# Running log-decay sums made once as rows, spread by single 512-column products

## What is computed

```python
# delta rule, per head
gc = jnp.cumsum(g, axis=-1)                      # g = -exp(a_log) * softplus(...)
decay = jnp.exp(jnp.where(causal, gc[..., :, None] - gc[..., None, :], -jnp.inf))
a_in = jnp.einsum("bhnid,bhnjd->bhnij", kb, k) * decay
qk = jnp.einsum("bhnid,bhnjd->bhnij", q, k) * decay
q_dec = q * jnp.exp(gc)[..., None]
...
# scan, per head
acs = jnp.cumsum(jnp.moveaxis(adt_i, 1, -1), axis=-1)
lmat = jnp.exp(jnp.where(causal, acs[..., :, None] - acs[..., None, :], -jnp.inf))
y_diag = jnp.einsum("bgls,bghls,bsghp->blghp", cb, lmat, xdt_i)
```

## Time and profile before

| what | us |
|---|---|
| median of 3 executions | 2161.22 |
| lowest, highest | 2158.73, 2166.72 |
| span of the profiled execution | 2157.8 |
| PE busy in it | 2109.7 (98%) |
| DVE, ACT, POOL busy | 1213.1, 906.3, 325.6 |

### The profile page before, as it was taken

One profiled execution on the slowest core, in us unless ns is written; L12 is line 12 of the kernel. 1 busy time (PEld: TensorE's weight loads), 2 busy tenths in 40 slices (PEclk: granted clock), 3 DMA queues, 4 the chain that ended last, 5 costly groups with the idle time before them and its releaser, 6 DMA issues.

```text
span 2157.8 us, 26841 instructions
## 1 busy us (share of the span) xinstructions
PE 2109.7 (98%) x9776; PEld 1698.0 (79%) x9776; DVE 1213.1 (56%) x1663; ACT 906.3 (42%) x1282; POOL 325.6 (15%) x266
## 2 busy tenths in 40 slices
PE   6999999999999999999999999999999999999999
PEld 5778888878868888877766888888878878888887
DVE  5898755765366665226544566653354465666522
ACT  6883445434254444224564444442242354444311
POOL 0002121220122222001302122210000011222100
PEclk9999999999999999999999999999999999999999
DMA  7323322122323233221111333232222122323321
GB/s 234 93 77 92 86 74 69 59 69 69 101 65 97 94 94 120 94 86 59 59 40 50 97 94 94 95 116 96 80 77 88 51 78 88 98 97 97 114 94 66
DMA packets 81481, 188.96 MB, mean 88 GB/s; under 512 B 19824, under 2 KB 40432, under 8 KB 81392
## 3 DMA queue, kind: packets, MB, share of 16 engines
q1 hardware_dynamic: 81392, 187.75, 27.6%
HBM read 178.28 MB, written 9.44 MB: 87 GB/s over the span
## 4 chain that ended last, share of the span: by engine, by line
PE 92%; DVE 4%; ACT 2%; issue 1%; DMA 0%; POOL 0%; SPq 0%; ACTq 0%; DVEq 0%; POOLq 0%
PE acc L253 23%; PE acc L255 23%; PE acc L254 23%; PE bank L1726 1%; PE bank L1245 1%; PE bank L229 1%; PE bank L230 1%; PE bank L231 1%; PE acc L2634 1%; PE acc L2633 1%; PE acc L2632 1%; PE bank L2017 1%; PE bank L253 1%; PE bank L255 1%; PE bank L254 1%
## 5 line engine op out<-in xcount | busy, mean ns | idle before, releaser
L253 PE MATMUL acc<-HH,whi 128*128 128x512 f32 x1600 | 642.1, 401 | 7.1 <-DVE wlo L191 4.5
L255 PE MATMUL acc<-HH,wlo 128*128 128x512 f32 x1600 | 624.4, 390 | 0.0
L254 PE MATMUL acc<-HL,whi 128*128 128x512 f32 x1600 | 623.5, 390 | 0.0
L185 ACT ACTIVATE whi<-raw 128x1024 fp32r<-128x1024 f32 (+1 forms) x293 | 324.2, 1108 | 573.5 <-PE acc L255 543.4
L191 DVE TENSOR_TENSOR wlo<-raw,whi 128x1024 fp32r<-128x1024 f32 (+1 forms) x293 | 400.9, 1369 | 287.8 <-ACT whi L185 287.8
L253 PEld LDWEIGHTS acc<-HH,whi 128*128 128x128 f32 x1600 | 301.1, 188 | 74.1 <-DVE wlo L191 11.0
L255 PEld LDWEIGHTS acc<-HH,wlo 128*128 128x128 f32 x1600 | 300.5, 188 | 64.0
L254 PEld LDWEIGHTS acc<-HL,whi 128*128 128x128 f32 x1600 | 301.1, 188 | 62.0 <-issue 4.1
L253 PE MATMUL acc<-FH,whi 128*128 128x512 f32 x528 | 208.9, 396 | 0.0
L255 PE MATMUL acc<-FH,wlo 128*128 128x512 f32 x528 | 208.6, 395 | 0.0
L254 PE MATMUL acc<-FL,whi 128*128 128x512 f32 x528 | 208.5, 395 | 0.0
(11 more groups left out here) (394 smaller groups left out, 2673.1 us busy)
## 6 DMA issues: line engine op xcount, KB each, us to landing
raw<-w SPq DMA_DIRECT2D x257, 512.0 KB, 3.5
raw<-w SPq DMA_DIRECT2D x48, 704.0 KB, 4.0
X<-x SPq DMA_DIRECT2D x4, 512.0 KB, 5.2
x_dram<-small SPq DMA_DIRECT2D x8, 256.0 KB, 4.4
xt_dram<-small SPq DMA_DIRECT2D x8, 256.0 KB, 3.6
a_dram<-l_am SPq DMA_DIRECT2D x8, 256.0 KB, 3.7
l_xt<-xt_dram SPq DMA_DIRECT2D x8, 256.0 KB, 3.5
l_x<-x_dram SPq DMA_DIRECT2D x8, 256.0 KB, 3.3
```

The lines of the kernel that those rows point to most:

```text
L185: nc.scalar.activation(hi[:, 0:kt * P], raw[u % RAW][:, 0:kt * P], ACT.Copy).then_inc(w_hi_ready, 1)
L253: nc.tensor.matmul(a[:, :], wh, tile(hi, k), start=start and k == 0, stop=False)
L254: nc.tensor.matmul(a[:, :], wh, tile(lo, k), start=False, stop=False)
L255: last = nc.tensor.matmul(a[:, :], wl, tile(hi, k), start=False, stop=stop and k == kt - 1)
```

## The change

The running sums of all 24 heads are made once, as rows. DVE writes `t_ld4`, which holds each chunk's 24 log-decay columns four times (signs -, -, +, + on the factor), POOL having zeroed it first. PE multiplies its four 128-column chunks by `upper` into `bank[5]` in the middle of the second unit of h = 1 (new L1448, four float32 128x128 products). ACT rounds the result into `rows_r` (fp32r); DVE replaces rows 32-63 and 96-127 of it with the remainders, so that a row and the row 32 below it add up to a sum in two rounded parts.

- Delta rule: L1764's four float32 products become one fp32r product of 512 columns, with `pick_r` (ones at rows p and 32+p) as stationary operand.
- Scan: POOL's `sd_u` becomes the chunk's rows times a selector of the head (`row_of`), with rows 64-127 set to one; the stationary operand is `sd_left` (ones above, the negative rows below). L2508's eight products become two of 512 columns. They give the difference of the sums with a sign that is not yet clamped, so ACT takes Abs from PSUM into `sd_e` and then Exp with scale -1, where it took one Exp.
- Once, ahead of the scan, POOL makes `row_of` in two steps and sets two memsets, and ACT copies half of `rows_r` to `sd_left`.
- The constant table is loaded in two pieces of 3 and 5 blocks of 128 columns instead of one of 13; seven thresholds on semaphores move with it.

The core of the diff:

```diff
+            dve.wait_ge(g_zero, 1)
+            for r, sign in enumerate((-1.0, -1.0, 1.0, 1.0)):
+                nc.vector.scalar_tensor_tensor(out=t_ld4[:, :].rearrange("p (c r n) -> p c r n", c=NC, r=4)[:, :, r, 0:24],
+                                               in0=by_chunk(t_soft)[:, :, 8:32], scalar=sign,
+                                               in1=t_neg[:, :].unsqueeze(1).to_broadcast([P, NC, 24]),
+                                               op0=ALU.mult, op1=ALU.mult).then_inc(a_dve, 1)
+
+        def rows_pe(pe):
+            pe.wait_ge(a_dve, 8)
+            for k in range(NC):
+                last = nc.tensor.matmul(chunk(bank[5], k), chunk(t_ld4, k), upper, start=True, stop=True)
+            last.then_inc(a_pe, 1)
+
+        def rows_act(act):
+            act.wait_ge(a_pe, 6)
+            nc.scalar.activation(rows_r[:, :], bank[5][:, :], ACT.Copy).then_inc(a_steps, 1)
+
+        def rows_dve(dve):
+            dve.wait_ge(a_steps, 9)
+            for r in (slice(32, 64), slice(96, 128)):
+                nc.vector.tensor_tensor(rows_r[r, :], bank[5][r, :], rows_r[r, :].bitcast(F32), ALU.subtract).then_inc(a_dve, 1)
...
+                if p == 0:
+                    rows_act(act)
                 act.wait_ge(unit_done, u0 + 2 * h + 2)
...
                     beta_exp_dve(dve)
+                    rows_dve(dve)
...
-                    unit(2 + 2 * h)
+                    unit(2 + 2 * h, 0)
+                    unit(2 + 2 * h, 1)
+                    rows_pe(pe)
+                    unit(2 + 2 * h, 2)
+                    unit(2 + 2 * h, 3)
                     pe.wait_ge(a_steps, 8)
...
-                    pe.wait_ge(a_dve, 4)
+                    pe.wait_ge(g_zero, 3)
+                    pe.wait_ge(a_dve, 11)
...
-                for k in range(NC):
-                    last = nc.tensor.matmul(chunk(bank[2], k), head_col(t_ld, 24 * k, p).to_broadcast([P, P]), upper,
-                                            start=True, stop=True)
-                last.then_inc(p_prod, 1)
+                nc.tensor.matmul(bank[2][:, :], pick_r[:, p:p + 1].to_broadcast([P, P]), rows_r[:, :],
+                                 start=True, stop=True).then_inc(p_prod, 1)
...
-                    nc.scalar.activation(sd_e[q][:, :], bank[q][:, :], ACT.Exp).then_inc(d_e, 1)
+                    nc.scalar.activation(sd_e[q][:, :], bank[q][:, :], ACT.Abs).then_inc(d_abs, 1)
+                for q in range(2):
+                    act.wait_ge(d_abs, 2 * n + q + 2)
+                    nc.scalar.activation(sd_e[q][:, :], sd_e[q][:, :], ACT.Exp, scale=-1.0).then_inc(d_e, 1)
...
-                    nc.gpsimd.tensor_tensor(by_chunk(sd_u[q]), of_heads(t_ld, 24 * k + 8 + 8 * g + 4 * q, 4, P),
-                                            each_chunk(lower), ALU.mult).then_inc(d_u, 1)
+                    h0 = 8 + 8 * g + 4 * q
+                    nc.gpsimd.tensor_tensor(by_chunk(sd_u[q]), each_chunk(chunk(rows_r, k).bitcast(F32)),
+                                            of_heads(row_of, h0, 4, P), ALU.mult).then_inc(d_u, 1)
...
-                    for j in range(4):
-                        last = nc.tensor.matmul(chunk(bank[q], j), chunk(sd_u[q], j), upper, start=True, stop=True)
-                    last.then_inc(d_d, 1)
+                    nc.tensor.matmul(bank[q][:, :], chunk(sd_left, k), sd_u[q][:, :], start=True, stop=True).then_inc(d_d, 1)
```

More of the change, by code:

```diff
@@ L95, in program @@
         ident, ones, upper, lower, halves = (cst[:, k * P:(k + 1) * P] for k in range(5))
-        neg_lower, neg_ones, hidden = (cst[:, k * P:(k + 1) * P] for k in range(12, 15))
-        level = [cst[:, (5 + k) * P:(6 + k) * P] for k in range(7)]
+        level = {5: cst[:, 5 * P:6 * P], 6: cst[:, 6 * P:7 * P]}
+        neg_lower, neg_ones, hidden = (cst[:, k * P:(k + 1) * P] for k in range(7, 10))
+        ident_half, row_of = cst[:, 10 * P:10 * P + 64], cst[:, 10 * P + 64:10 * P + 96]
         def col(name, k=0, n=1):
@@ L1666, in inverse_dve @@
                 dve.wait_ge(blk_in, 16 * heads_until(batch))
-                dve.wait_ge(g_zero, 4 if batch == 2 else 2)
+                dve.wait_ge(g_zero, 6 if batch == 2 else 4)
             for j in range(j0, j1):
@@ L1718, in prep_pool @@
         def prep_pool(pool, c):
+            nc.gpsimd.memset(t_ld4[:, :], 0.0).then_inc(g_zero, 1)
             nc.gpsimd.memset(l_inv[:, :], 0.0).then_inc(g_zero, 1)
-            pool.wait_ge(g_zero, 1)
+            pool.wait_ge(params_in, ALL_PARAMS)
+            nc.gpsimd.tensor_tensor(pick_r[:, :], ident[:, 0:8], ident[:, 32:40], ALU.add).then_inc(g_zero, 1)
+            pool.wait_ge(g_zero, 2)
             pool.wait_ge(z_filled, 32 * NH)
@@ L2235, in program @@
             ("st", 29, 1)))
-        sd_u, sd_e, sd_sq = ([at_tile(f"sd_{n}{j}", k + j) for j in range(2)] for n, k in (("u", 21), ("e", 23), ("sq", 30)))
+        sd_e, sd_sq = ([at_tile(f"sd_{n}{j}", k + j) for j in range(2)] for n, k in (("e", 23), ("sq", 30)))
+        sd_u = [place(f"sd_u{j}", S, FREE + (21 + j) * TILE, F32R) for j in range(2)]
+        sd_left = place("sd_left", S, tab0 + (664 * 4 + LINE - 1) // LINE * LINE, F32R)
         sd_sq += [at_tile(f"sd_sq{j}", 15 + j) for j in (2, 3)]
+        d_pick, d_abs = sem("ssd_pick_ready"), sem("ssd_left_abs_ready")
         d_u, d_xdd, d_scaled = sem("ssd_u_ready"), sem("ssd_xdd_ready"), sem("ssd_state_scaled")
@@ L2330, in gate @@
                 nc.scalar.activation(sd_t[:, :], sd_t[:, :], ACT.Exp, scale=-0.5).then_inc(d_rs, 1)
+            act.wait_ge(c_t, NH)
+            nc.scalar.activation(sd_left[64:P, :], rows_r[64:P, :], ACT.Copy).then_inc(d_abs, 1)
             for k in range(2):
@@ L2471, in u_of @@
                         pool.wait_ge(d_d, 2 * (n - 1) + q + 1)
-                    nc.gpsimd.tensor_tensor(by_chunk(sd_u[q]), of_heads(t_ld, 24 * k + 8 + 8 * g + 4 * q, 4, P),
-                                            each_chunk(lower), ALU.mult).then_inc(d_u, 1)
+                    h0 = 8 + 8 * g + 4 * q
+                    nc.gpsimd.tensor_tensor(by_chunk(sd_u[q]), each_chunk(chunk(rows_r, k).bitcast(F32)),
+                                            of_heads(row_of, h0, 4, P), ALU.mult).then_inc(d_u, 1)
             pool.wait_ge(g_o, NH)
+            nc.gpsimd.tensor_tensor(ident_half, ident[:, 0:64], ident[:, 64:P], ALU.add).then_inc(d_pick, 1)
+            pool.wait_ge(d_pick, 1)
+            nc.gpsimd.tensor_tensor(row_of, ident_half[:, 0:32], ident_half[:, 32:64], ALU.add).then_inc(d_pick, 1)
+            pool.wait_ge(d_pick, 2)
+            nc.gpsimd.memset(sd_left[0:64, :].bitcast(F32), 1.0).then_inc(d_pick, 1)
+            pool.wait_ge(d_pick, 3)
+            pool.wait_ge(d_abs, 1)
+            nc.gpsimd.memset(rows_r[64:P, :].bitcast(F32), 1.0).then_inc(d_pick, 1)
+            pool.wait_ge(d_pick, 4)
             u_of(0, 0)
@@ L2506, in decays @@
                         pe.wait_ge(d_e, 2 * (n - 1) + q + 1)
[L2507 to L2509 removed]
+                    else:
+                        pe.wait_ge(d_abs, 1)
+                        pe.wait_ge(d_pick, 4)
+                    nc.tensor.matmul(bank[q][:, :], chunk(sd_left, k), sd_u[q][:, :], start=True, stop=True).then_inc(d_d, 1)
             def start(g):
```

18 lines of the change are left out of this document (11 added, 7 removed).

## The result

The changed kernel takes 2144.03 us, the median of 6 executions (2142.23 to 2147.19), against 2160.89 for 6 of the kernel before (2158.73 to 2166.72). The ratio is 0.991, its interval 0.9892 to 0.9929: 0.9% faster, where I had forecast 0.34% and a range that ended at 2148.0. The profiled executions have spans of 2157.8 and 2140.9 us, 16.9 apart. The forecast explains less than half of that, and one row of the page says where to look for the rest. Five of the six executions before lie at 2158.7 to 2161.2; beside the experiments the same kernel comes out near 2167 more often than near 2159, with the granted clock. At equal clock (table under Experiments) the change gains 23.3 to 23.7 us, 1.1%.

A forecast was written before the change was run, and what follows sets the result against it. PE, busy 98% of the span, was taken as the bound, with DVE setting the preparation's end. Terms -0.75 - 8.68 + 2.1 gave -7.3 us: span 2150.5, median 2153.9 us (0.34% faster), range 2148.0 to 2159.0.

The forecast's parts named there:

- POOL, SP and the rest: POOL's `sd_u` and preparatory steps, ACT's copy into `sd_left`, the table's two loads: 0 us, within 0.5 either way.
- Delta rule, one head: PE in heads 1 to 7: one fp32r product for L1764's four saves 0.66 us a head.
- Head 0: Delta rule's head 0: the four new products cost PE +0.89 us; what L1764 loses here gains nothing.
- What survives the preparation: End of the delta rule's preparation: only 0.75 us earlier, because DVE's full stretch sets the end.
- the other bound: Preparation if all seven heads kept their savings on PE: 7 x 0.66 - 0.89 = 3.73 us earlier.
- rival A: Preparation: DVE's full stretch gives way, heads 4 to 7 keep 0.66 us each; -10.3 us in all, 2150.9; chance 10%.
- Scan, PE's part: L2508's groups on PE: 1.24 us saved in each of seven, n = 1 to 7, 8.68 us in all.
- Scan, ACT's part: Abs plus Exp delays `sd_xdt` 1.05 us in n = 0 and n = 4, +2.1 us; the other six chunks are covered.
- Rival C: Scan's six middle chunks: ACT's longer chain makes PE wait at L2556, 1.05 us each; +6.4 us, 2167.6; chance 3%.
- Rival D: fp32r products with broadcast or half-constant operands run at float32 pace, saving nothing; +3.0 us, 2164.2; chance 2%.
- The sum: Whole kernel: -0.75 - 8.68 + 2.1 = -7.3 us, span 2157.8 to 2150.5.
- Rival B, the clock: Longer PE waits bring one or two more half-clock stretches, 1.7 us each: -5.6 or -3.9 us, 2155.6 to 2157.3; chance 17%.

The follow-up runs named there:

- experiment 1: Changed kernel with its scratch region back at the old start, byte 126208: 2160.51 us, ratio 0.9976 to the kernel before.
- experiment 2: Kernel before with its scratch region 128 bytes lower, at byte 126080, and the smaller constant table loaded in two pieces: 2148.71 us, ratio 0.9916.
- experiment 5: Changed kernel, old region start, one part each: first delta rule's alone, 2167.17 us (0.9995 to before); then scan's alone, 2161.36 us (0.9982).
- experiment 6: Changed kernel with the two Abs of each group's first chunk moved ahead of the last SiLU: 2141.77 us, ratio 0.988 to the kernel before.
- experiment 3: Kernel before, smaller table, old region start: first, weights moved 128 bytes, 2174.01 us (1.004); second, X, HH and HL moved 128 bytes, 2188.45 us (1.0105).
- experiment 4: Kernel before, smaller table, scratch region at byte 125824, then 126144, then 126112: spans 2152.3, 2156.6 and 2168.4 us.

## Why the prediction was wrong

**The step that failed is "POOL, SP and the rest".** There I priced the smaller table as two loads and took 0. That the table, `rows_r` and `pick_r` are buffers in a row, and that everything behind them moves, was in the diff and was not in my sum. 13.7 us hang on it in the kernel before, 15 to 16 in the changed one (experiments 1 and 2). In the two traces of the changed kernel 1.2 us of that are a stretch of half clock at 631 us that lasts 3.4 us with the new start and 6.8 with the old; the rest of the difference is open. No mechanism among the rivals had it.

**Delta rule, one head**: 0.66 us forecast, 0.67 measured. **Head 0**: +0.89 forecast, +0.81 measured. **What survives the preparation**: -0.75 forecast from DVE's full stretch, -0.86 measured, and the whole part alone is 0.1 to 0.8 us faster. The -3.73 of the other bound did not come; rival A is refuted by DVE's row and by experiment 5.

**Scan, PE's part**: 1.24 us a group forecast, 1.28 measured over n = 1 to 4 and 1.25 over n = 5 to 7. **Scan, ACT's part**: +1.05 twice forecast, +1.06 and +0.89 measured, and taken away again by experiment 6. Rival C is refuted: PE never waits in the middle chunks. Rival D too: the broadcast product takes 0.23 us [compare rows 2].

**The sum** of these terms is -7.8 in the shifts and -7.4 to -8.8 at equal clock, against -7.3.

**Rival B, the clock**, came true in its mechanism between the two profiled executions, and on top of the forecast. I gave it 17% and "one or two more such stretches" of 1.7 us. The two traces have 5.5 us of it: +0.86 before the heads, +3.04 in n = 4, +1.57 at 631 us. Two steps of its working failed. The size: such a stretch lasts 3.4 or 6.8 us here, and 6.8 us of full work at half clock cost up to 3.4. And the evidence against it, "a wait of 1.78 us passed at full clock": one execution had shown it so, and in experiment 5 the same wait was followed by half clock. How much of it the change causes, one pair of traces can't say: the profiled execution before had a clock of 0.998, which 10 of the 45 reach, and other traces with the old scan, that of experiment 2 and the first of experiment 5, have 6.8 us of half clock in n = 4 and 3.4 us at 640 us too. Over many executions the sign holds and the size is less. Of 30 with the scan's new form and none of the waits shortened or filled (the changed kernel, experiment 1, the scan's part of experiment 5) none had a mean clock above 0.995; of 55 with its old form (the kernel before, the delta rule's part) 18 did. The changed kernel's mean is 0.0011 below that of the kernel before, by the step above 1 to 2 us. So the clock hid a little of what the layout brought.

**The range** had no room for an unpriced cause of that size, and took the spread of the runs as noise, where most of it goes with the granted clock of an execution.

## What to carry to other kernels

Before pricing a diff, recompute the addresses: a buffer that grows or shrinks moves everything allocated behind it, and here 128 bytes were worth twice what the edit was made of. Let stationary and moving operand start at the same place modulo 256 bytes. Compare executions at equal granted clock where the effect is below 1%, and don't take one profiled execution as proof that a wait of 2 to 3 us leaves the clock alone. Products whose results nobody reads, put into such a wait, cost nothing here.

## What the runs showed of the hardware

- fp32r products of 128x128 weights with 128x512 data follow each other by 226.7 to 227.5 ns when both operands start at the same place modulo 256 bytes, and by 232.4 to 233.4 ns when they are 128 or 32 bytes apart; 64 bytes apart it was 228.9 ns in the mean. The full difference is 2 to 3% of PE's time in a loop that is nothing but products.
- The clock fell from 2.4 to 1.2 GHz in or just behind waits of PE of 1.8 to 3.7 us, for 3.4 or 6.8 us, in some executions and not in others. With the waits filled it also fell at 175.7 us, where the waits just before were 1.06 and 0.69 us; at this place three traces (the second kernel of experiment 3, the first and third of experiment 4) have 10.2 us of it.
- ACT took Abs between SiLUs and between Exps without a further table load: 54 loads in the kernel before, in the changed one and in experiment 6.
- POOL's first two tiles of `sd_u` took 2.04 us and take 2.68 us in the new form, but the median of all 16 tiles is 1.04 us in both. It is covered, as forecast.

```profile
370.43 2.68 POOL L2518 TENSOR_TENSOR sd_u<-rows_r,cst 128x512 fp32r<-128x512 f32 x2 [4.88 <-PE bank L2565]
```
